# Final norm of a two-block transformer on one core: sums spread by a matrix of ones, Sqrt on ScalarE, reciprocal on VectorE, stores from two queues

## What is computed

```
def _rmsnorm(x, g):
    xf = x.astype(jnp.float32)
    y = xf * lax.rsqrt(jnp.mean(xf * xf, axis=-1, keepdims=True) + EPS)
    return (y * g.astype(jnp.float32)).astype(x.dtype)
...
        h = _rmsnorm(x, ffn2_norm[i])
        x = x + 0.5 * _swiglu(h, ffn2_w_gate[i], ffn2_w_up[i], ffn2_w_down[i])
    return _rmsnorm(x, final_norm)
```

## Time and profile before

| | us |
|---|---|
| median of 3 runs (1230.91 to 1232.11) | 1231.02 |
| the profiled execution, its own time | 1231.67 |
| its span, first to last instruction | 1229.7 |
| PE busy | 1219.6 (99%) |
| DVE busy | 867.6 (71%) |
| ACT busy | 684.1 (56%) |
| POOL busy | 152.4 (12%) |

### The profile page before, as it was taken

How to read it: one execution, slowest core, us unless ns; L and a number is a source line. 1 busy time by engine, 2 the same in 40 slices (tenths; PEclk the granted TensorE clock), 3 DMA queues, 4 the chain that set the end, 5 groups by cost and what they waited for, 6 DMA issues and landing times.

```text
span 1229.7 us, 24147 instructions
## 1 busy us (share of the span) xinstructions
PE 1219.6 (99%) x10076; PEld 1149.3 (93%) x10076; DVE 867.6 (71%) x1375; ACT 684.1 (56%) x1107; POOL 152.4 (12%) x209
## 2 busy tenths in 40 slices
PE   8999999999999999999999999999999999999997
PEld 7889888999999988899999999999998889999997
DVE  6999799787675567777676556667546777766742
ACT  7566566655554475565555445455456556555541
POOL 4201500373001200021000100000120003000001
PEclk9999999999999999999999999999999999999998
DMA  8545645566555554446655656565555434665550
GB/s 317 190 147 187 215 138 164 179 192 218 192 185 193 188 174 135 135 134 213 194 182 192 191 184 208 190 204 194 190 170 185 137 122 138 207 205 193 185 189 35
DMA packets 61388, 221.09 MB, mean 180 GB/s; under 512 B 7264, under 2 KB 7392, under 8 KB 61024
## 3 DMA queue, kind: packets, MB, share of 16 engines
q1 hardware_dynamic: 60768, 218.87, 54.1%
q0 software_dynamic: 224, 0.53, 0.2%
q10 hardware_dynamic: 288, 0.16, 0.0%
HBM read 218.48 MB, written 1.05 MB: 179 GB/s over the span
## 4 chain that ended last, share of the span: by engine, by line
PE 89%; issue 7%; POOL 2%; DMA 1%; ACT 0%; SPq 0%; DVE 0%; POOLq 0%; ACTq 0%
PE pb L495 13%; PE pb L496 13%; PE pb L497 13%; PE pb L475 8%; PE pb L477 8%; PE pb L476 8%; PE pb L510 6%; PE pb L512 6%; PE pb L511 6%; PE pb L577 3%; PE pb L606 1%; PE pb L634 1%; POOL s_ssum L1895 1%; POOL s_sq L1892 1%; DMA s_wraw<-in_w 1%
## 5 line engine op out<-in xcount | busy, mean ns | idle before, releaser
L1242 DVE TENSOR_TENSOR s_wl<-s_wraw,s_wh 128x1024 fp32r<-128x1024 f32 (+1 forms) x411 | 501.7, 1242 | 120.9 <-ACT s_wh L886 120.4
L886 ACT ACTIVATE s_wh<-s_wraw 128x1024 fp32r<-128x1024 f32 (+1 forms) x411 | 419.8, 1048 | 189.3 <-PE pb L497 83.0
L495 PE MATMUL pb<-s_xh,s_wh 128*128 128x256 f32 x1296 | 359.1, 277 | 0.0
L497 PE MATMUL pb<-s_xh,s_wl 128*128 128x256 f32 x1296 | 358.3, 276 | 0.0
L496 PE MATMUL pb<-s_xl,s_wh 128*128 128x256 f32 x1296 | 358.3, 276 | 0.0
L496 PEld LDWEIGHTS pb<-s_xl,s_wh 128*128 128x128 f32 x1296 | 243.5, 188 | 0.0
L495 PEld LDWEIGHTS pb<-s_xh,s_wh 128*128 128x128 f32 x1296 | 243.5, 188 | 0.0
L497 PEld LDWEIGHTS pb<-s_xh,s_wl 128*128 128x128 f32 x1296 | 243.4, 188 | 0.0
L510 PE MATMUL pb<-s_hh,s_wh 128*128 128x256 f32 x660 | 182.2, 276 | 0.0
L511 PE MATMUL pb<-s_hl,s_wh 128*128 128x256 f32 x660 | 182.2, 276 | 0.0
L512 PE MATMUL pb<-s_hh,s_wl 128*128 128x256 f32 x660 | 182.2, 276 | 0.0
(11 more groups left out here) (325 smaller groups left out, 1552.7 us busy)
## 6 DMA issues: line engine op xcount, KB each, us to landing
s_wraw<-in_w SPq DMA_DIRECT2D x407, 512.0 KB, 4.1
s_nab<-in_rpb SPq DMA_DIRECT2D x2, 1024.0 KB, 8.9
s_x<-in_x SPq DMA_DIRECT2D x4, 256.0 KB, 6.0
out_dram<-s_at_s SPq DMA_DIRECT2D x4, 256.0 KB, 2.6
s_cst<-in_cst SPq DMA_DIRECT2D x1, 680.0 KB, 10.3
s_wraw<-in_w SPq DMA_DIRECT2D x2, 256.0 KB, 4.2
s_ln<-in_lng POOLq DMA_DIRECT2D x2, 128.0 KB, 6.7
s_ln<-in_lnb POOLq DMA_DIRECT2D x2, 128.0 KB, 8.0
```

What stands on the lines that cost most here:

```text
L495: pe.matmul(o, wh[:, s, w], xk[0], start=k == v == 0, stop=False, skip_group_check=True)
L497: r = pe.matmul(o, wl[:, s, w], xk[0], start=False, stop=k == 7, skip_group_check=True)
L886: return act.activation(o, src, ACT.Copy, scale=scale)
L1242: dve.tensor_tensor(wl[:, s, part], wraw[:, r, part], wh[:, s, part].bitcast(F32), ALU.subtract).then_inc(low_done, 1)
```

## The change

The last squares are now multiplied by a full 128x128 matrix of ones (`spread_sums` in place of `norm_sums(END, 1)`, `spread_last_sums` in place of the four L876 matmuls). Every partition then holds the sum of every token, so the two spreads, `mean_squares(END)` and `root(END)` go. ACT takes the root with scale 1/D and a bias tile holding epsilon, straight from PSUM into `ssum`. DVE inverts it in place. All four multiplies now read `ssum` in SBUF. ACT issues the stores 2 and 1 on its own queue, SP the stores 0 and 3. A one-element Sqrt stands before the last squares on ACT. `posf` grows from two to four columns to hold epsilon; the SBUF addresses of all other tiles stay as they were.

```diff
@@ bank_plan, tiles @@
-    for name in ("sum", "last", "last2"):
-        use(END, name, 4 + turn % 4)
-        turn += 1
+    use(END, "sum", 4 + turn % 4)
...
-    posf = sb("posf", [P, 2])
+    posf = sb("posf", [P, 4])
+    eps = posf[:, 2:4]
+    posf = posf[:, 0:2]
@@ pe_program @@
+        def spread_sums():
+            pe.wait_ge(sum_done, sum_count(END, 0))
+            pe.matmul(claim(END, "sum")[:, 0:TOKENS], cview("ones", P), ssum[:, :], start=True, stop=False)
+
+        def spread_last_sums():
+            o = psum(END, "sum")[:, 0:TOKENS]
+            for v in range(2):
+                pe.wait_ge(last_sq, v + 1)
+                r = pe.matmul(o, cview("ones", P), sq[:, 1, TOKENS * v:TOKENS * (v + 1)], start=False, stop=v == 1)
+            r.then_inc(*fill(END, "sum"))
...
             if n == END - 1:
-                norm_sums(END, 1)
+                spread_sums()
                 tiles(n, 132)
...
-        for c in range(2 * TOKENS // P):
-            if c % 2 == 0:
-                pe.wait_ge(last_sq, c // 2 + 1)
-            r = pe.matmul(o[:, 2 * (c % 2):2 * (c % 2) + 2], sq[:, 1, P * c:P * (c + 1)], ones, start=False, stop=c > 1,
-                          skip_group_check=True)
-        r.then_inc(*fill(END, "sum"))
-        spread(END, "last", NORM[END], rms_count(END))
-        spread(END, "last2", NORM[END], rms_count(END))
+        spread_last_sums()
@@ act_program, next_input @@
                     if q < 3:
                         act.wait_ge(*gone(n, ("out", q)))
+                    else:
+                        act.wait_ge(eps_done, 1)
+                        act.activation(eps[:, 1:2], eps[:, 0:1], ACT.Sqrt)
...
-                act.wait_ge(*full(END, "last2"))
-                copy(ssum[:, :], psum(END, "last2")[:, 0:TOKENS]).then_inc(last_kept, 1)
+                act.wait_ge(*full(END, "sum"))
+                act.activation(ssum[:, :], psum(END, "sum")[:, 0:TOKENS], ACT.Sqrt, bias=eps[:, 0:1], scale=1.0 / D).then_inc(
+                    last_root, 1)
+                for q in (2, 1):
+                    act.wait_ge(last_done[q], 1)
+                    act.dma_start(out[:, NCOL * q:NCOL * (q + 1)], flat(y[:, 2 * q:2 * q + 2, :])).then_inc(st_out, 16)
@@ dve_program @@
         dve.memset(junk[:, :, :], 0.0).then_inc(junk_done, 1)
+        dve.memset(eps[:, :], EPS).then_inc(eps_done, 1)
...
-        mean_squares(END)
-        dve.wait_ge(*full(END, "last"))
+        dve.wait_ge(last_root, 1)
+        dve.reciprocal(ssum[:, :], ssum[:, :]).then_inc(last_kept, 1)
+        dve.wait_ge(last_kept, 1)
...
-            dve.tensor_tensor(yq, yq, psum(END, "last")[:, 0:TOKENS].unsqueeze(1).to_broadcast([P, 2, TOKENS]),
-                              ALU.mult).then_inc(last_done[q], 1)
+            dve.tensor_tensor(yq, yq, ssum[:, :].unsqueeze(1).to_broadcast([P, 2, TOKENS]), ALU.mult).then_inc(last_done[q], 1)
@@ pool_program, sp_program @@
-        root(END)
...
-        for q in (0, 2, 1, 3):
+        for q in (0, 3):
             sp.wait_ge(last_done[q], 1)
```

More of the change, by code:

```diff
@@ L341, in program @@
     sq_done, pair_done, sum_done, last_sq = sem("sq_done"), sem("pair_done"), sem("sum_done"), sem("last_sq")
-    last_x, last_kept = sem("last_x"), sem("last_kept")
+    last_x, last_root, last_kept, eps_done = sem("last_x"), sem("last_root"), sem("last_kept"), sem("eps_done")
     ms_done, rms_step, rs_done, gfg_done = sem("ms_done"), sem("rms_step"), sem("rs_done"), sem("gfg_done")
@@ L589, in norm_sums @@
                     c = 4 * kind + 2 * t
-                    r = pe.matmul(o[:, c:c + 2], sums_at[kind][:, P * t:P * (t + 1)], ones, start=c == 0, stop=n != END,
+                    r = pe.matmul(o[:, c:c + 2], sums_at[kind][:, P * t:P * (t + 1)], ones, start=c == 0, stop=True,
                                   skip_group_check=True)
-            if n != END:
-                r.then_inc(*fill(n, "sum"))
+            r.then_inc(*fill(n, "sum"))
+        def spread_sums():
[7 more added lines that the diff above has]
+            r.then_inc(*fill(END, "sum"))
         def spread(n, name, row, ready):
@@ L869, in pe_program @@
                 feed(n)
-        ones = cview("ones", 2)
-        o = psum(END, "sum")
-        for c in range(2 * TOKENS // P):
-            if c % 2 == 0:
-                pe.wait_ge(last_sq, c // 2 + 1)
-            r = pe.matmul(o[:, 2 * (c % 2):2 * (c % 2) + 2], sq[:, 1, P * c:P * (c + 1)], ones, start=False, stop=c > 1,
-                          skip_group_check=True)
-        r.then_inc(*fill(END, "sum"))
-        spread(END, "last", NORM[END], rms_count(END))
-        spread(END, "last2", NORM[END], rms_count(END))
+        spread_last_sums()
     def act_program(act):
```

## The result

The changed kernel takes 1232.88 us in the median of 20 runs, the kernel before 1231.13 in the same comparison: 1.75 us more, a ratio of 1.0013 with a 95% interval from 1.0007 to 1.0019. One of the changed kernel's 20 runs took 1517.9 us at a mean granted clock of 0.757, where the others have 0.996 to 0.998; the ratio leaves it out, and without it the median is 1232.84 and the difference 1.71. So it is slower by an amount that 20 runs of each can resolve, and within the 0.2% that the prediction called "the same". The forecast was 1232.3.

A forecast was written before the change was run, and what follows sets the result against it. PE bounds until 1220.5, then the closing chain and stores; multiplies starting 0.54 later, turns and stores move the span's end from 1229.70 to 1231.06, +1.36, say 1.3, on 1231.02: 1232.3 us, by itself 1231.9 to 1232.9, with rivals 1230.3 to 1233.4.

The forecast's parts named there:

- PE ahead of the end: Before the last squares' sum, four norm_sums records (0.50 us) become two of 256 columns (0.60), costing 0.1 us on PE.
- The sum: Last matmul of the squares' sum on PE: starts 1221.47, takes 0.60, ends 1222.07 against 1222.09; nothing lost or gained.
- The root: Sqrt on ACT from PSUM after the last matmul: 0.475 us from 1222.15 to 1222.63, its table load covered earlier.
- The reciprocal: DVE's inversion of 256 elements before the multiplies: 1.58 us at 5.6 ns per element, ends 0.42 and 2.0.
- The turns: DVE and POOL alternate at SBUF in the final multiplies, ending at 0.63, 1.90, 2.53 and 3.16 after their start.
- The stores: After the multiplies: store 2's data starts at t0 + 3.47, three stores run 2.1, tail 1.1, end t0 + 6.67.
- t0: The forecast's start of the final multiplies, 1224.39 us including PE's 0.1, which is 0.54 later than before the change.
- multiplies before 1223.9: Sign at the final multiplies: if DVE's start before 1223.9, the prediction is wrong in kind.
- the dearer reciprocal: Rival for DVE's inversion: 8.5 ns per element, 2.34 us, change costs 2.1 us, time 1233.1; chance 20%.
- the plain one: Rival for DVE's inversion: plain operation rate, 0.42 us, change costs 0.1 us, time 1231.2; chance 14%.
- No turns: Rival for the final multiplies: POOL and DVE overlap as before, change costs 0.2 us, time 1231.2; chance 11%.
- The slow landing on ACT's queue: Rival for the final stores: ACT's last store takes 4.3 us to land, costing 2.5 us, time 1233.6; chance 5%.

The follow-up runs named there:

- the factor in PSUM: The changed kernel with the inverted root copied to PSUM by DVE, whose three multiplies read it there: 1232.33 us, ratio 1.0004 to the kernel before.
- the run with two queues: The kernel before with only the stores changed, SP issuing 0 and 3, ACT 2 and 1: 1231.59 us, ratio 0.9999.
- the narrow root: The kernel before with the root of its two sum columns by Sqrt on ACT and a two-column reciprocal on DVE: 1230.56 us, ratio 0.9993.

## Why the prediction was right, and by how much it missed

The forecast held in kind, and each of its steps has a measured counterpart. In the forecast the tail grows by 1.26 (1.36 less the 0.1 that falls to PE ahead of it); it grew by 1.55. Of the 0.29 between them 0.22 lie ahead of the multiplies and 0.07 behind their start.

- **PE ahead of the end.** `spread_sums` was to cost 0.1, and cost nothing. The chain gives it 0.43 where the four records before had 0.34, but the matmul behind it takes 0.12 where it took 0.22. From the start of the last matmul ahead (L526) to that of the second one behind (L525) it is 0.66 after and 0.68 before. The chains, before and after:

```profile
1215.83 0.34 PE pb L590 x4
1216.17 0.22 PE pb L524
```
```profile
1215.30 0.43 PE pb L596 x2
1215.73 0.12 PE pb L524
```

- **The sum.** Forecast 0.60 for the last matmul, measured 0.70, so it ends at 1221.63. The root starts 1.66 after the second add where I had 1.60, but not for that reason: the chain goes through ACT's gain copies, which end as late after the second add as before the change (1.67), and the 0.07 that I took off for overlap did not show. PE's clock was full, as forecast.
- **The root.** 0.475 forecast, 0.47 measured, with no table load in front of it; the load ran at 1207.67, behind the last unit of weights, as the order had said.
- **The reciprocal**, the term with the widest bounds: 1.58 forecast from two rows of four elements, between 0.42 and 2.0; 1.75 measured. These 0.17 are the largest part of the miss. The reading of the earlier trace rows was right in kind, a price for each element well above the plain one: 5.6 ns forecast, 6.25 measured. That it came so near is in part luck. It rests on 18 ns between two medians, while the reciprocals of that row alone spread from 158 to 178; the fastest against 154 would have given 2.1 ns and 0.68 us.
- **The turns.** Three DVE multiplies and POOL's were to take 3.16 and took 2.96: POOL needs 1.12 between two of DVE's, not 1.27. Their order was the one forecast.
- **The stores.** From the start of the multiplies to the end 6.67 forecast, 6.74 measured. That is luck: two errors cancel in it. The turns were 0.20 shorter, and a store takes 0.77 of DMA time, not 0.70. The 0.70 came from the fastest window; the whole stretch of the earlier trace rows, from 1225.43 to about 1228.6 with one dip, already had 0.75 for each store. The forecast named the waiting for quarter 2 but not the hole in the data that comes from it, though its own sum holds one (store 0's data ends at t0 + 2.27, store 2's starts at t0 + 3.47).

The sign "multiplies before 1223.9" was nearly met, with 1223.96, only because the second add came 0.55 earlier in this execution; positions from the start of the span were the wrong scale for it.

Of the rivals, the dearer reciprocal (2.34) and the plain one (0.42) both fell with the 1.75 measured. "No turns" fell with the trace of the change and with the factor in PSUM. The slow landing on ACT's queue fell: its two stores landed in 2.5 to 3.0, SP's in 2.4 to 3.4. Eight times the plain rate, one of them, would be 8.5 ns for each element; this case shows 6.25. The Trainium skill (VectorE: DVE Perf Modes, section First, the fixed hardware budget) gives the reciprocal a repeat count of 8 but no time, and no run here shows how the two are related.

The difference of the medians, 1.71 to 1.75 us, is some 0.2 more than that of the two tails, 1.55. With a spread of 1.5 to 2 us among runs of one kernel, this is not resolved. One thing could account for it: the profile of the kernel before has its spreads at half the clock, and an execution in which they ran faster, as in the run with two queues, would have a tail shorter by some 0.16. How often that happens, no run shows.

## What to carry to other kernels

A reciprocal on DVE cost 6.25 ns for each element of a row here, nearly six times the 1.07 of an operation with two SBUF inputs, so invert while the data is still narrow (two columns took 0.17 us) and broadcast afterwards; a wide matrix of ones that spares two spreads can cost more than it spares. When DVE and POOL share the elements of one step, let DVE take one input from PSUM, or leave POOL out: with two SBUF inputs on DVE, four multiplies on DVE alone were faster than three and one. Once stores of known size stand at the end, count from the first issue and look for holes in the data before adding a queue: four whole stores without a hole ended 4.9 to 5.15 us after the first issue in five different kernels (the one before the change among them, with a dip of some 0.16).

## What the runs showed of the hardware

- A multiply-add on DVE with one SBUF input and 256 f32 elements took 0.29 us, where the copy of as many from SBUF to PSUM took 0.43.
- PE's granted clock fell to half after very different idle times. Before the change it was 0.55 in the window from 1222.5, with PE idle since 1222.09. After the change, with PE idle since 1221.63, it was still full in the window from 1224.0 to 1224.5 and 0.71 in the next:

```profile
1224.00:1224.50 0.50, 0.00 (x0) 1.00 0.00 0
1224.50:1225.00 0.50, 0.00 (x0) 0.71 0.00 0
```

So the price of the two spreads is no fixed number: after the same pause of 1.04 they took 1.13 in one execution and 0.97 in another, and 0.67 in the narrow root, where PE paused for 0.55 and the clock read 1.00.
